# A hybrid diffusion block on one core: the columns of w_ada split at three quarters instead of a half

## The reference, cut to what matters

```python
sc, scc = jax.nn.silu(c), jax.nn.silu(c_ctx)
mod_l = jnp.split((sc @ w_ada[i] + b_ada[i])[:, None, :], 6, axis=-1)
mod_c = jnp.split(scc @ w_ada[i] + b_ada[i], 6, axis=-1)
hl = rmsnorm(xl, norm1_w[i]) * (1 + mod_l[1]) + mod_l[0]      # 512 latent tokens x 2048
hc = rmsnorm(xc, norm1_w[i]) * (1 + mod_c[1]) + mod_c[0]      # 256 context tokens x 2048
# token_mixers: p, q, ff, fb, i, og, gp, gh = split_in(h @ w_in)
#   f = lb + (1 - lb) * sigmoid(z_ff or z_fb);  k = 1 - f;  v = z_i
#   context: the two gated scans (forwards and backwards) give a 128x128 state for each of 8 heads
#   latents: the same scans, started from the context's states, then branches, w_out, and the
#   grouped top-2 mixture of experts (16 experts, 2048 -> 512 -> 2048), final rmsnorm
```

## Time and profile before

| | us |
|---|---|
| median of 3 runs (2249.31 to 2251.55) | 2251.29 |
| the profiled execution's own time | 2252.37 |
| its span | 2250.8 |
| PE busy | 2165.2 (96%) |
| DVE busy | 1559.2 (69%) |
| ACT busy | 992.6 (44%) |
| POOL busy | 527.4 (23%) |

### The profile page before, as it was taken

One profiled execution on the slowest core, in us unless ns is written; L12 is line 12 of the kernel. 1 busy time (PEld: TensorE's weight loads), 2 busy tenths in 40 slices (PEclk: granted clock), 3 DMA queues, 4 the chain that ended last, 5 costly groups with the idle time before them and its releaser, 6 DMA issues.

```text
span 2250.8 us, 36334 instructions
## 1 busy us (share of the span) xinstructions
PE 2165.2 (96%) x12392; PEld 1765.7 (78%) x12392; DVE 1559.2 (69%) x1944; ACT 992.6 (44%) x1216; POOL 527.4 (23%) x670
## 2 busy tenths in 40 slices
PE   4889999999999999999999999999899999999997
PEld 2679878887887887788888888788678888888884
DVE  3478555666567656766666766743688989889898
ACT  3344323233233324322222222333268888888882
POOL 0046435553554354111111111100010010100101
PEclk9999999999999999999999999999889999999999
DMA  9965563222222223777677766834499999999996
GB/s 388 401 207 157 154 205 87 84 86 86 77 86 86 84 86 98 212 226 249 213 221 250 217 222 213 274 126 150 167 366 407 417 414 421 418 419 418 416 407 225
DMA packets 324463, 531.36 MB, mean 236 GB/s; under 512 B 12432, under 2 KB 247440, under 8 KB 294704
## 3 DMA queue, kind: packets, MB, share of 16 engines
q1 hardware_dynamic: 290976, 393.91, 49.0%
q0 software_dynamic: 33424, 136.62, 16.9%
HBM read 493.74 MB, written 36.73 MB: 236 GB/s over the span
## 4 chain that ended last, share of the span: by engine, by line
PE 81%; DVE 4%; issue 2%; DMA 1%; POOL 1%; ACT 0%; DVEq 0%; ACTq 0%; POOLq 0%; SPq 0%
PE ps L715 13%; PE ps L717 12%; PE ps L716 12%; PE ps L1068 7%; PE ps L1070 7%; PE ps L1069 7%; PE ps L946 3%; PE ps L947 3%; PE ps L948 3%; PE ps L1005 2%; PE ps L1007 2%; PE ps L1006 2%; PE ps L1094 1%; PE ps L825 1%; DVE e_lo L2278 1%
## 5 line engine op out<-in xcount | busy, mean ns | idle before, releaser
L1665 DVE TENSOR_TENSOR w_lo<-raw,w_hi 128x1024 fp32r<-128x1024 f32 x272 | 349.4, 1285 | 356.3 <-ACT w_hi L1228 354.7
L1228 ACT CAST w_hi<-raw 128x1024 fp32r<-128x1024 f32 x272 | 285.1, 1048 | 583.6 <-PE ps L717 277.9
L715 PE MATMUL ps<-hl_hi,w_hi 128*128 128x512 f32 x1280 | 505.8, 395 | 3.7 <-DVE hl_lo L1731 1.4
L717 PE MATMUL ps<-hl_hi,w_lo 128*128 128x512 f32 x1280 | 498.8, 390 | 0.0
L716 PE MATMUL ps<-hl_lo,w_hi 128*128 128x512 f32 x1280 | 498.6, 390 | 0.0
L2120 DVE TENSOR_TENSOR e_lo<-e_raw,e_hi 128x1024 fp32r<-128x1024 f32 x357 | 421.5, 1220 | 44.1 <-ACT e_hi L1509 36.9
L1509 ACT CAST e_hi<-e_raw 128x1024 fp32r<-128x1024 f32 x357 | 369.1, 1058 | 72.4 <-PE ps L1070 72.3
L715 PEld LDWEIGHTS ps<-hl_hi,w_hi 128*128 128x128 f32 x1280 | 240.3, 188 | 54.8 <-issue 3.4
L717 PEld LDWEIGHTS ps<-hl_hi,w_lo 128*128 128x128 f32 x1280 | 240.2, 188 | 50.8
L716 PEld LDWEIGHTS ps<-hl_lo,w_hi 128*128 128x128 f32 x1280 | 240.5, 188 | 47.9
L1068 PE MATMUL ps<-e_hi,xe_hi 128*128 128x512 f32 x512 | 201.2, 393 | 0.1
(11 more groups left out here) (387 smaller groups left out, 3591.8 us busy)
## 6 DMA issues: line engine op xcount, KB each, us to landing
e_raw<-in_w_e SPq DMA_DIRECT2D x192, 1024.0 KB, 9.6
raw<-in_w_in SPq DMA_DIRECT2D x208, 512.0 KB, 3.9
ada<-in_w_ada POOLq DMA_DIRECT2D x64, 1024.0 KB, 6.5
ada_ring<-in_w_ada SPq DMA_DIRECT2D x32, 1024.0 KB, 16.1
raw<-in_w_out SPq DMA_DIRECT2D x32, 512.0 KB, 4.3
block_outputs<-y_sb POOLq DMA_DIRECT2D x30, 512.0 KB, 6.7
block_outputs<-osq POOLq DMA_DIRECT2D x1, 8192.0 KB, 27.8
raw<-in_w_branch_hgrn SPq DMA_DIRECT2D x16, 512.0 KB, 3.8
```

The costliest lines, as they stand in the source:

```text
L715: mm(dst, hi, rhs_hi[:, k, :], start=(k == 0), stop=False)
L717: last = mm(dst, lo, rhs_hi[:, k, :], start=False, stop=(k == KT - 1))
L1228: act_e.copy(w_hi[:, hslot, :], raw[:, slot, :]).then_inc(hi_done, 1)
L1665: tt(w_lo[:, hslot, :], raw[:, slot, :], w_hi[:, hslot, :].bitcast(F32), ALU.subtract).then_inc(split_done, 1)
```

## The change

The split of the 4096 columns moves from one half to three quarters. The first group has columns 0 to 1535 of shift and of scale (`WIDE`), in 16 slots of one row block (1.57 MB in one DMA); the second has the last 512 columns of each, in 4 slots of four row blocks (2.1 MB in four DMAs). The first group gives row blocks 0 to 11, the second 12 to 15. So 18 units are early instead of 12 (six for each tile, heads 0 to 3, row blocks 0 to 11). The last four row blocks of heads 0 to 3 are taken by pairs of heads in six units (`pair_products`), and heads 4 to 7 keep their six units each. The heads 0 to 3 are thus complete at units 20 and 23 (two heads each); the scans, evacuations and transposes are given to units by tables (`C_KEYS`, `C_EV`, `C_STATE`) and not by the unit's own head. The tiles of heads 5 and 7 get banks of their own. `ctx_keys` reads `lb_all` directly and drops the small copy to `lb_v` or `lb_p`.

```diff
-        ada_ring = Room(nc, base, 10, 74).new("ada_ring", [P, 4, 2, 2048], F32)
+        ada_ring = Room(nc, base, 10, 74).new("ada_ring", [P, 4, 4096], F32)
...
-        ADA_HALF = KT // 2
+        N_ADA = KT + 4
+        WIDE = 3 * D // 4
...
-        N_EARLY = 3 * EARLY
-        C_STATE = (18, 22, 25, 29, 32, 38, 44, U_H + 1)
+        EARLY_PIECES = 6
+        N_EARLY = 3 * EARLY_PIECES
+        C_REST = N_EARLY + 6
+        C_STATE = (24, 28, 31, 35, 38, 42, 46, U_H + 1)
+        C_EV = ((18, 19, 20), (21, 22, 23), (24, 25, 26), (27, 28, 29), (30, 31, 32), (34, 35, 36), (38, 39, 41),
+                (43, 45, 47))
+        C_KEYS = (18, 21, 24, 28, 31, 35, 39, 43)
+        HL_AT = {22: 2, 27: 3, 32: 4, 37: 5, 41: 6, 46: 7}
...
             def ada_rows(q):
+                pe.wait_ge(ada_in[q % 4], 16 * (q // 4 + 1) if q < KT else 128)
+                if q < KT:
+                    for b in range(6):
+                        m, n = (b // 2, b % 2) if b < 4 else (b - 4, 2)
+                        c0 = 32 * (b % 4)
+                        last = mm(ps[c0:c0 + 2, OB + b // 4, :], cs[:, :, q],
+                                  ada_ring[:, q % 4, m * WIDE + n * 512:m * WIDE + (n + 1) * 512], start=(q == 0),
+                                  stop=(q == KT - 1), tile_position=(0, c0))
...
-            for q in range(5, ADA_HALF):
+            for q in range(5, KT):
                 ada_rows(q)
             turn_mod(0)
...
-            for q in range(ADA_HALF, KT):
-                n = 2 * (q - ADA_HALF)
-                for s in range(n, min(n + 2, N_EARLY)):
+            for i in range(4):
+                for s in range(3 * i, 3 * i + 3):
                     quad_products(s)
-                ada_rows(q)
+                ada_rows(KT + i)
+            quad_products(12)
             turn_mod(1)
+            for s in range(13, N_EARLY):
+                quad_products(s)
             for s in range(N_EARLY, U_H):
...
-                ctx_products(s)
+                if s < C_REST:
+                    pair_products(s)
+                else:
+                    ctx_products(s)
...
             def mod_out(g):
...
+                    if g == 0:
+                        act_e.copy(mod01_row[rows, 1, :], ps[rows, UB, :])
+                        last = act_e.copy(mod01_row[rows, 0, :], ps[rows, OB, :])
...
+                for h in range(HEADS):
+                    n = s - C_KEYS[h]
+                    if n == 0:
                         ctx_keys(h)
+                    elif h < EARLY and n in (1, 2):
+                        ctx_levels(h, *((1, 3), (4, 8))[n - 1])
+                    elif h >= EARLY and n in (1, 2, 3):
+                        ctx_levels(h, *((1, 2), (3, 5), (6, 8))[n - 1])
+                if s == 20:
+                    for n in range(EARLY_PIECES, CTX_PIECES):
+                        modulate(xT_lat, n, 0)
+                if s in HL_AT:
+                    hl_lo_piece(HL_AT[s])
```

More of the change, by code:

```diff
@@ L566, in _ @@
             sp.dma_start(masks_in[:], level_masks).then_inc(consts_in, 16)
-            for s in range(N_EARLY + 1, U_H):
+            for s in range(12, U_H):
                 load_ctx(s)
@@ L734, in quad_products, with pair_products @@
                 last.then_inc(units_done, 1)
+            def pair_products(s):
+                hp, i = pair_unit(s)
+                pe.wait_ge(split_done, split_value(s))
+                for z in range(2):
+                    for kk in range(4):
+                        k = 2 * EARLY_PIECES + kk
+                        if s == N_EARLY and z == 0 and kk % 2 == 0:
+                            pe.wait_ge(h_split, k // 2 + 1)
+                        at = kk * 2 * P + z * P
+                        hi, lo = (w[:, s % 2, at:at + P] for w in (w_hi, w_lo))
+                        dst = ctx_bank(2 * hp + z, i)
+                        mm(dst, hi, hc_hi[:, k, :], start=False, stop=False, skip_group_check=True)
+                        mm(dst, hi, hc_lo[:, k, :], start=False, stop=False, skip_group_check=True)
+                        last = mm(dst, lo, hc_hi[:, k, :], start=False, stop=(k == KT - 1), skip_group_check=True)
+                last.then_inc(units_done, 1)
             def ctx_products(s):
@@ L738, in ctx_products @@
                 dst = ctx_bank(h, i)
-                if s >= N_EARLY and h:
-                    pe.wait_ge((c_sig_f, c_sig_b, c_v_ev)[i], h)
+                if half == 0:
+                    pe.wait_ge((c_sig_f, c_sig_b, c_v_ev)[i], (2, 4, 5, 6)[h - EARLY])
                 pe.wait_ge(split_done, split_value(s))
@@ L1286, in _ @@
                         act_e.copy(c_vT[:, h % 2, :], ctx_bank(h, 2)).then_inc(c_v_ev, 1)
[L1287 to L1288 removed]
+                if s in HL_AT:
+                    hl_hi_piece(HL_AT[s])
             def mix(hd, idx):
@@ L1708, in _ @@
             dve.wait_ge(xT_dve, 2 * (NTOK + NCTX))
-            for n in range(4):
+            for n in range(EARLY_PIECES):
                 modulate(xT_ctx, n, 1)
@@ L1732, in hl_lo_piece @@
                    hl_hi[:, 2 * n:2 * n + 2, :].bitcast(F32), ALU.subtract).then_inc(h_split, 1)
+            for s in range(14, N_EARLY + 1):
+                w_lo_unit(s)
+                if s in (14, 15):
+                    modulate(xT_ctx, EARLY_PIECES + s - 14, 1)
+                if s in (15, 16):
+                    ctx_lo(EARLY_PIECES + s - 15)
+                if s >= 17:
+                    hl_lo_piece(s - 17)
             def ctx_keys(h):
-                own.wait()
-                own.did(dve.tensor_copy(lb_v[:], lb_all[:, h, :]))
                 own.wait()
```

184 lines of the change are left out of this document (94 added, 90 removed).

## The result

The changed kernel takes 2259.59 us, median of 6 runs (2257.93 to 2261.14), against 2250.64 for the kernel before, median of 6 (2248.95 to 2251.55). The ratio is 1.0038 (95% interval 1.0027 to 1.0048); by the medians it is slower by 8.95 us. The forecast of 2255.6 is 4.0 us too low, the range held the time, and the change came out on the side of slower (0.45), not on the one that I held likeliest (the same, 0.48). The profiled execution took 2259.65 us, its span is 2258.0.

The account below looks back on a forecast made before the run. DMA taken to bound the start, PE the stretch behind it: first product 23.9 us later, stretch 19.6 less, latent stage 4.3 later; 2252.37 profiled becomes 2256.7, less 1.1 to the median: 2255.6 us, range 2249.5 to 2262.

Parts of the forecast that it names:

- the stretch: From the first product to the latent stage: 166.9 us instead of 186.5, 19.6 less.
- the late slot: Last w_ada slot of the second group: PE's wait for it, 2.0 us before, goes.
- the second modulation: Modulation behind the second w_ada group: 5.0 us before, goes under PE's units; two transposes stay, 0.3.
- DVE's queue: Units 18 to 47: PE waits on DVE, 4.0 us in all, 3.2 of it on w_lo ahead of unit 22.
- the wait ahead of the third unit: Early units: the third w_lo stands behind two more modulated pieces, + 0.3 us.
- rival D: Units pass faster than 2.97 us where nothing stands between them; a gain of 4.5 us needs 8.9 off 166.9; 4%.
- The gap at 26 us: Opening: DMA engines run dry before the fourth token tile's bytes come, between nothing and 2.9 us, taken as 1.7.
- both kernels have the same list: From the latent stage's start on: nothing changes, 1994.9 us kept, a shift of the start taken one to one.
- the signs of being wrong: First product before 91 or after 96, DVE waits over 7 or under 1, clock under 1 before 85, 1994.9 us not kept.
- Rival A: PE at 1.2 GHz: last w_ada slot + 1.7, transposes + 0.5, unit 22 + 2.3 us; sign: clock under 1, 70-85 us; 18%.
- B: POOL's heads all run at 13.1 us, so PE waits on them: + 2.8 us, 2258.4; 10%.
- the second seam: Break before products resume behind the second w_ada group: 5.0 us of modulation and 2.8 of lower clock, both go.

Follow-up runs that it names:

- the five slots: Changed kernel with five slots of 1.57 MB instead of four for the first 16 parts of w_ada: 2255.07 us, 1.0015 of the kernel before.
- The padded pair: Semaphore increments ahead of PE's first wait, schedule untouched: changed kernel with 143, 2267.52 us; kernel before with 113, 2258.89 us.
- the kernel with both edits: Changed kernel with five w_ada slots and the latents' last two modulations moved to units 16 and 17: 2253.08 us, 1.0010 of the kernel before.
- everything mended on both sides: Changed kernel with five slots, earlier modulations, costless pad: 2251 to 2252 us, not run; kernel before with late transposes, no lb_all copies, earlier hl_lo: 2244.43 us.
- the three padded ones: Changed kernel with 143 increments, 2267.52 us; kernel before with 113, 2258.89; changed kernel with 143, five slots and earlier modulations, 2260.79.

## Why the prediction was right or wrong

**Right in its frame.** PE bounds the stretch and the DMA engines the start, and most terms of the stretch came out: slots of 256 columns in 1.91 us for 1.83, no wait on POOL, none on the late slot, 3.0 for 3.2 us ahead of unit 22, the second modulation without a stall. The remaining 0.8 for DVE's queue did not come.

**The total of the stretch is nearer than its parts.** It took 165.4 us for 166.9 predicted, but two misses cancel. The sum has no term for the lower clock behind the wait at unit 22 (1.5 us) and only 0.3 for the wait ahead of the third unit (0.9). On the other side the units pass faster where they stand in a row, the mechanism of rival D in a small size. The first of nine such units, ahead of the wait at 173.65:

```profile
144.46 0.36 PE L758 MATMUL ps<-hc_hi,w_hi 128*128 128x256 f32 x1
```

From there to the beginning of the wait, 173.65 - 2.98 = 170.67, it is 26.2 us, 2.91 a unit for 2.97 predicted.

**Wrong in size: the step "So the DMA engines run dry there until the new transfer's first bytes come ... and take 1.7".** The gap at 26 us was 2.0. But the term was sized as one gap, and there is a second one (54 to 58 us at 189 instead of 410 GB/s, 54% of 4 us, 2.2), because I asked only how much stood ahead of the token tiles and not what the ring holds while PE turns them: 4 x 1.57 = 6.3 MB now, 8.4 before. 2.0 + 2.2 - 1.7 = 2.5 of the 3.5 us by which the last slot is late; the rest is a rate of 399 to 409 GB/s instead of 410, and the landing. That the ring's depth counts was shown by the five slots: with 7.9 MB the spell at 26 us goes and 2.1 us of DMA time are lost in all, and only the 8.4 MB of the kernel before have no spell. The first dry spell depends on the depth too: in the second trace of the kernel before, too, SP issued the fourth tile late (27.23 us), and the DMA share from 26 to 28 us stayed at 1.03.

**Wrong: "both kernels have the same list" behind the latent stage.** The list is the same, its place in PE's program is not: + 3.0 us in the last stage. That is 2.7 of waiting and 1.8 for the lower clock behind it, less 1.4 that the down products ran faster. The padded pair shows the wait without the clock: both have the lower clock in the down products and not behind them, and differ by 3.2 us (54.3 and 51.1), 2.8 of it the wait. It was not among my rivals, only among the signs of being wrong. The Trainium skill (Runtime: NRT & Kernel Launch, Instruction fetch mechanics) says that a taken branch whose target is outside the blocks already fetched has to wait for a fetch. The traces agree: a packet of instructions arrives in each of the six waits, which took 2.5 to 2.8 us.

**Rival A was partly right.** Two of its places showed the lower level (1.2 GHz): the slot at 71.78 took 3.55 us, hidden as worked out, and the two units behind the wait at 173.65 took 7.3 us (to 180.98) instead of 5.8, 1.5 us on the path; the clock of that stretch returned to 1.00 when the wait shrank. The last slot and the transposes ran at the full level. So A's own sign came (a granted clock of 0.89 from 70 to 85 us in both traces), and 1.5 of its 4.5 us. Slots of 1.9 us of work every 3.8 mostly kept the clock. I had applied the rule that I cited there (the Trainium skill, TensorE: Matmul & The Clock Gate, HAM oscillation — how this bites in real kernels) to a case it doesn't describe: it speaks of work that is shorter than the wait for its data, and here work and wait were level (1.89 us each at the last slots). In this trace the slots at the lower level stood behind longer waits, 4.78 and 3.31 us. In the kernel with both edits a slot behind 1.09 us took 3.58 too, so the length of the wait ahead of a slot doesn't decide alone.

**What luck had in it.** The range reached to 2262 for the sake of rivals A and B, the lower clock and POOL. POOL cost nothing and the clock a third of its price; the second dry spell and the jump took their place, and neither had a term. By my own signs the prediction was wrong in three places: a first product after 96 us (96.28 and 97.31), a granted clock under 1 ahead of 85 us, and a part behind the latent stage's start that didn't keep its length.

**Why it doesn't pay.** 8.39 MB ahead of the first product cost 20.5 us at 410 GB/s. What they can bring back on PE is 7.3 (four slots' worth of `ada_rows` now hidden in the opening), 5.0 + 2.8 (the second seam) and 2.0 (the late slot), 17.1 in all. The start is later by 26.9 (20.5, the dry spells 4.2, the seam 1.3, the rest rate and landing) and the stretch is shorter by 21.1. The 4.0 us on POOL that the change also saves are a matter of the due times alone, as the kernel before with later transposes shows. Smaller gains (1.4 and 1.7 us of waits gone, units that pass faster) and losses (3.0 and 1.5 at unit 22, 0.9 at the third unit) nearly cancel. With everything mended on both sides it would be 2251 to 2252 us (estimated above) against 2244.4 (measured), so the split itself costs some 7 us.

## What to carry to other kernels

Bytes moved ahead of the first product cost their full time at the DMA rate; they pay only where the seam and the hidden work behind it are longer than that. When a ring's slots change in size, count what it holds while its consumer is busy elsewhere. And a change at the front moves every later instruction in the engine's program: if the end of a trace changes where the list didn't, look for a wait on nothing behind a jump.

## What the runs showed of the hardware

- A forward jump of PE over 373 instructions cost nothing when it ended, counted in blocks of 256 from the program's start, in the next block (as from 9504 to 9877; eight traces), and 2.5 to 2.8 us when it ended one block further (9617 to 9990; six traces). In those six a 16.4 KB packet of instructions arrives during the wait.
- A semaphore increment on PE took some 0.15 us (4.54 us for 30).
- A ring of slots for w_ada lost no DMA time behind 26 us with 8.4 MB (share 1.02), 2.1 us with 7.9 MB and 3.7 or more with 6.3 MB, on the same token tiles.
- The lower clock falls in one of two places of the last stage: in the 48 down products (12.6 us instead of 11.2) in all unpadded kernels with the split at a half and in the three padded ones, or in the eight matmuls behind the wait (5.40 instead of 3.70) in three of the five traces of unpadded kernels with the change; in the two others in neither (last stage 52.4 us). What decides between them stays open.
